# First modulation chunks in four column pieces, the first projection multiplied with them

## The reference

```
mod = silu(c) @ w_ada + b_ada                    # 1024 -> 6 * 1024
shift1, scale1, gate1, shift2, scale2, gate2 = split(mod, 6)
h = rms_norm(x, norm1_g) * (1 + scale1) + shift1
z = h @ w_in                                     # q_a k_a v_a f_a q_b k_b v_b g_a g_b
q_a, k_a, q_b, k_b: rms_norm per head of 64
y_a = attention with forget gates from f_a; y_b = attention with linear biases (8 heads each)
x = x + gate1 * ((sigmoid(g_a) * (y_a @ w_up_fox) + sigmoid(g_b) * (y_b @ w_up_moba)) @ w_out)
h2 = rms_norm(x, norm2_g) * (1 + scale2) + shift2
x = x + gate2 * peer_ffn(h2)                     # 8 heads x 16 experts per token, rows gathered
```

## Time and profile before

| | |
|---|---|
| time, median of 3 runs | 903.43 us (902.26 to 903.75) |
| profiled execution, first to last instruction | 901.5 us |
| mean granted TensorE clock | 0.980 |
| first projection (QA) starts | 31.67 us |
| second projection (VA) starts | 49.42 us |
| attention, VectorE's first partials | 113.73 us |

### The profile page before, as it was taken

The page is one execution under the profiler, slowest core; times in us unless marked ns, Lnnn a source line. Parts: engine busy times, 40 slices in busy tenths (PEclk is TensorE's granted clock), DMA queues, the critical chain, the costliest instruction groups (busy, mean ns, idle before and its releaser), DMA issues.

```text
span 901.5 us, 8445 instructions
## 1 busy us (share of the span) xinstructions
PE 774.0 (86%) x2526; PEld 417.5 (46%) x2526; DVE 613.4 (68%) x1420; ACT 346.4 (38%) x1027; POOL 286.3 (32%) x279
## 2 busy tenths in 40 slices
PE   4999999999999999999997778787777777777777
PEld 2477877667556566565652333233322233222232
DVE  6788798963587977848669788758744444444445
ACT  3458688872243342423423242322422222222222
POOL 4000000000244445453537344453343333333320
PEclk9999999999999999999999989999999999999999
DMA  9978454679399999999999999999999999999994
GB/s 374 422 268 293 165 206 190 251 308 406 109 376 423 418 421 422 416 422 422 420 421 422 421 422 419 422 422 421 423 420 423 420 422 421 421 422 421 422 421 202
DMA packets 44100, 336.70 MB, mean 373 GB/s; under 512 B 4884, under 2 KB 5012, under 8 KB 7320
## 3 DMA queue, kind: packets, MB, share of 16 engines
q0 software_dynamic: 37152, 268.45, 71.8%
q1 hardware_dynamic: 6888, 67.72, 19.1%
q10 hardware_dynamic: 16, 0.00, 0.0%
HBM read 335.11 MB, written 1.05 MB: 373 GB/s over the span
## 4 chain that ended last, share of the span: by engine, by line
PE 49%; DMA 36%; DVE 10%; ACT 3%; issue 2%; SPq 0%; DVEq 0%; ACTq 0%
DMA ring<-in_peer_uv,eid 28%; PE ps_y L1625 21%; PE bank L1595 6%; DMA rows<-in_peer_uv,eid 4%; DMA extra<-in_peer_uv,eid 4%; PE bank L1561 3%; DVE ring L1019 2%; PE bank L1436 2%; PE bank L1438 2%; PE bank L1437 2%; PE bank L1576 2%; PE ps_y L1436 1%; PE ps_y L1438 1%; PE ps_y L1437 1%; PE ps_y L1400 1%
## 5 line engine op out<-in xcount | busy, mean ns | idle before, releaser
L1625 PE MATMUL ps_y<-ring,diag 128*128 128x512 f32 x572 | 275.5, 621 | 57.5 <-ACT diag L1311 57.5
L590 POOL DMA_INDIRECT ring<-in_peer_uv,eid x142 | 156.4, 1102 | 419.8 <-DVE eid L925 228.3
L1019 DVE CUSTOM_DVE_ANT_0 ring<-ring,gates 128x1024 f32<-128x1024 f32 x143 | 173.3, 1225 | 100.4 <-DMA ring<-in_peer_uv,eid 99.7
L1625 PEld LDWEIGHTS ps_y<-ring,diag 128*128 128x128 f32 x572 | 109.4, 197 | 205.5 <-issue 118.8
L1299 ACT ACTIVATE mask<-mask 128x2 f32<-128x2 f32 (+1 forms) x132 | 26.7, 202 | 364.1 <-DVE mask L1019 364.0
L1311 ACT ACTIVATE diag<-ident,mask 128x128 f32<-128x128 f32 x256 | 87.3, 386 | 0.3
L1625 PE MATMUL ps_y<-rows,diag 128*128 128x512 f32 x136 | 63.6, 611 | 9.6 <-ACT diag L1311 9.6
L1304 ACT ACTIVATE mask<-g_sb,mask 128x1 f32<-128x1 f32 x256 | 61.9, 287 | 4.3
L1019 DVE CUSTOM_DVE_ANT_0 rows<-rows,gates 128x1024 f32<-128x1024 f32 x34 | 41.2, 1224 | 31.1 <-DMA rows<-in_peer_uv,eid 31.0
L654 DVE TENSOR_TENSOR w_lo<-ring,w_hi 128x512 fp32r<-128x512 f32 x76 | 50.7, 685 | 11.5 <-PE bank L1438 10.0
L1115 ACT ACTIVATE w_hi<-ring 128x512 fp32r<-128x512 f32 x76 | 45.5, 626 | 24.4 <-PE bank L1438 23.9
(11 more groups left out here) (230 smaller groups left out, 1192.7 us busy)
## 6 DMA issues: line engine op xcount, KB each, us to landing
ring<-in_ada_t SPq DMA_DIRECT2D x11, 2048.0 KB, 9.7
ring<-in_in_t SPq DMA_DIRECT2D x10, 2048.0 KB, 10.3
ring<-in_up_t SPq DMA_DIRECT2D x2, 2048.0 KB, 8.7
ring<-in_out_t SPq DMA_DIRECT2D x2, 2048.0 KB, 13.7
ring<-in_peer_uv,eid POOLq DMA_INDIRECT x142, 28.9
x_sb<-in_x SPq DMA_DIRECT2D x2, 1024.0 KB, 12.1
ring<-in_ada_t SPq DMA_DIRECT2D x2, 1024.0 KB, 21.4
kz<-in_peer_t SPq DMA_DIRECT2D x1, 2048.0 KB, 23.4
```

The source lines that it names most:

```text
L590: pool.indirect_dma_start(uv_row(n), None, peer_uv, bass.IndirectOffsetOnAxis(ap=eid[:, n:n + 1], axis=0)).then_inc(s_uv[name], 16)
L1019: dve.tensor_tensor_reduce(u_row(n), u_row(n), h2[:, n // P, :], 1.0, 0.0, ALU.mult, ALU.add, adot[:, at:at + 1]).then_inc(s_dot, 1)
L1625: ins = pe.matmul(ps_y[:, cut], diag[:, n % ND, :], v_row(n)[:, cut], start=first, stop=last)
```

## The change

The columns of the first four modulation chunks are reordered on the host, so that piece j holds shift1 and scale1 for the k-blocks 2j and 2j+1 of h. A piece is made directly as columns: VectorE now sums 7 k-blocks (6 in the last piece), `piece_sum` turns and sums them with four matmuls that have the partials as stationary operand and one moving column, and `piece_direct` does the remaining k-block (two in the last piece) in the same way from the ring. VectorE reduces the pieces' columns from PSUM and makes `mod` and `a1` for two k-blocks; ScalarE makes those four blocks of h (both tiles) and rounds them. TensorE multiplies them at once with a quarter of QA's weights, all in plain fp32 (`PLAIN = 8`), and the forget logits are accumulated piece by piece in `ps_y`. QA's weights are loaded in four quarters, one behind each modulation chunk; modulation 0 is loaded to slot 3 and modulation 3 follows it there once it is summed. The two scalings of x move from VectorE to ScalarE, two memsets from GpSimd to VectorE. Modulation 4's partials move from QA to KA; modulation 5's from KA to QB (3), KB (3) and VB (2), and its row is summed in attention's step 1. The order of loads behind the head gives modulation 6 the slot of modulation 5.

```diff
-ADA_PE = ((5, 6, 7), (5, 6, 7), (5, 6, 7), (3, 6, 7))
-PLAIN = 4
+PIECE_PE = ((7,), (7,), (7,), (6, 7))
+PLAIN = 8
-ADA_DURING = {QA: 4, KA: 5}
+ADA_DURING = {KA: ((4, 0, 8),), QB: ((5, 0, 3),), KB: ((5, 3, 6),), VB: ((5, 6, 8),)}
+ADA_ROW_AFTER = {QB: 4}
-ADA_LATE = {3: 6, 6: 7, 10: 8, 14: 9, 16: 10}
+ADA_LATE = {1: 5, 3: 6, 6: 7, 10: 8, 14: 9, 16: 10}
...
-    chunks = [("ada", n) for n in range(ADA_FIRST)]
-    chunks += [("z", QA), ("z", VA), ("ada", 4), ("z", KA), ("ada", 5), ("z", QB), ("z", KB), ("z", VB)]
+    pieces = [("ada", 0), ("z", QA), ("ada", 1), ("ada", 2), ("ada", 3)]
+    slot_of = dict(zip(pieces, (3, 0, 1, 2, 3)))
+    chunks = [("z", VA), ("z", KA), ("ada", 4), ("z", QB), ("ada", 5), ("z", KB), ("z", VB)]
     chunks += [("z", 6), ("ada", 6), ("z", 7), ("ada", 7), ("z", 8), ("ada", 8), ("ada", 9), ("z", 9), ("ada", 10), ("ada", 11)]
     chunks += [("up", 0), ("up", 1), ("out", 0), ("out", 1)]
+    slot_of.update(zip(chunks, (1, 2, 3, 0, 1, 2, 3, 0, 1, 2, 3, 0, 1, 2, 3, 0, 1, 2, 3, 0, 1)))
...
+            for j in range(ADA_FIRST):
+                key = ("ada", j)
+                if held_by[key] is not None:
+                    await_chunk_read(sp, held_by[key])
+                for h in range(2):
+                    half = slice(h * KD // 2, (h + 1) * KD // 2)
+                    sp.dma_start(ring[:, slot_of[key], half, :], ada_t[j, :, half, :]).then_inc(s_piece[j][h], 16)
+                two = slice(2 * j, 2 * j + 2)
+                sp.dma_start(ring[:, slot_of["z", QA], two, :], in_t[QA, :, two, :]).then_inc(s_first[j], 16)
...
-            for n in (slice(0, 3), slice(4, 5)):
-                pool.memset(rows[:, n, :], 0.0).then_inc(s_zero, 1)
...
+            for n in (slice(0, 3), slice(4, 5)):
+                dve.memset(rows[:, n, :], 0.0).then_inc(s_zero, 1)
...
+            for j in range(ADA_FIRST):
+                piece(j, 0, PIECE_PE[j][0])
+                if j:
+                    h_low(j - 1)
+                to = columns_of(mod[:], j)
+                parts = len(PIECE_PE[j]) + 1
+                dve.wait_ge(s_summed, j + 1)
+                link(dve.tensor_reduce(to, ps_y[:, 16 * j:16 * j + 4 * parts].rearrange("p (s a k) -> p a k s", a=2, k=2),
+                                       AX_X, ALU.add))
+                link(dve.tensor_tensor(to, to, columns_of(cols[:, 24:24 + 2 * KD], j), ALU.add))
...
+            h_low(ADA_FIRST - 1)
+            low_parts(KD, KD + NLO)
...
+                    for n, first, last in ADA_DURING.get(c_, ()):
+                        m = first + k - (KD - (last - first))
+                        if m >= first:
+                            partials(n * KD + m, n * KD + m + 1)
...
+            for j in range(ADA_FIRST):
+                act.wait_ge(s_a1, j + 1)
+                for k in (2 * j, 2 * j + 1):
+                    for t in range(TILES):
+                        key = ("xT", t, k // 4)
+                        ins = act.activation(hT[:, k, t * P:(t + 1) * P], bank(key)[:, (k % 4) * P:(k % 4 + 1) * P],
+                                             ACT.Identity, scale=a1[:, k:k + 1], bias=mod[:, k:k + 1])
...
+                h_high(j)
...
+            def piece_direct(j):
+                pe.wait_ge(s_piece[j][1], 16)
+                for part, k in enumerate(PIECE_PE[j]):
+                    for m in range(4):
+                        pe.matmul(piece_cols(j, part + 1)[:, m:m + 1], ring[:, slot_of["ada", j], k, m * P:(m + 1) * P],
+                                        silu[:, k:k + 1], start=True, stop=True)
+            def piece_sum(j):
+                pe.wait_ge(s_acc, j + 1)
+                for m in range(4):
+                    ins = pe.matmul(piece_cols(j, 0)[:, m:m + 1], sums_first[:, j % 2, m * P:(m + 1) * P],
+                                    ones[:, 0:1], start=True, stop=True)
+                ins.then_inc(s_summed, 1)
...
+            piece_direct(0)
             for t in range(TILES):
...
+            for j in range(ADA_FIRST):
+                if j:
+                    piece_direct(j)
+                piece_sum(j)
+                if j:
+                    forget_part(j - 1)
+                first_part(j, first_spots)
+            forget_part(ADA_FIRST - 1)
```

More of the change, by code:

```diff
@@ L511, in _ @@
                 sp.dma_start(rows[0:1, r, :], b_ada[0:1, at * D:(at + 1) * D]).then_inc(s_bias, 16)
-            for n in range(ADA_FIRST, len(chunks)):
-                chunk(n)
+            for key in chunks:
+                chunk(key)
             await_block(sp, NZ * KD - 1)
@@ L652, in low_parts @@
                         await_block(dve, j - NLO)
-                    w = ring[:, chunk_no["z", n] % NW, k, :]
+                    w = ring[:, slot_of["z", n], k, :]
                     dve.tensor_tensor(w_lo[:, j % NLO, :], w, w_hi[:, j % NHI, :].bitcast(F32),
                                       ALU.subtract).then_inc(s_w_lo, 1)
[L657 to L665, removed]
-                        continue
[L667 to L672, removed]
@@ L675, in _, with piece @@
-            middle = slice(ADA_FIRST - 1, ADA_FIRST)
-            link(dve.memset(pads, 0.0))
-            link(dve.memset(pads[:, KD, middle], 1.0))
+            def piece(j, first, last):
+                acc = sums_first[:, j % 2, :]
+                for k in range(first, last):
+                    w = ring[:, slot_of["ada", j], k, :]
+                    if k == 0:
+                        dve.wait_ge(s_piece[j][0], 16)
+                        if j >= 2:
+                            dve.wait_ge(s_summed, j - 1)
+                        link(dve.tensor_scalar(acc, w, silu[:, 0:1], None, ALU.mult))
+                        continue
+                    if k == KD // 2:
+                        dve.wait_ge(s_piece[j][1], 16)
+                    ins = dve.scalar_tensor_tensor(out=acc, in0=w, scalar=silu[:, k:k + 1], in1=acc,
+                                                   op0=ALU.mult, op1=ALU.add)
+                    if k + 1 in PIECE_PE[j]:
+                        ins.then_inc(s_acc, 1)
+                    else:
+                        link(ins)
@@ L696, in _ @@
[L696 to L714, removed]
+            inverse_root(D, TILES, s_rstd)
+            for j in range(ADA_FIRST):
[8 more added lines that the diff above has]
+                link(dve.tensor_tensor(to, to, columns_of(cols[:, 24:24 + 2 * KD], j), ALU.add))
+                two = slice(2 * j, 2 * j + 2)
+                dve.scalar_tensor_tensor(out=a1[:, two], in0=mod[:, KD + 2 * j:KD + 2 * j + 2], scalar=1.0,
+                                         in1=cols[:, KD + 2 * j:KD + 2 * j + 2],
+                                         op0=ALU.add, op1=ALU.mult).then_inc(s_a1, 1)
@@ L769, in _ @@
             dve.wait_ge(s_bias, 4 * 16)
[L770 to L774, removed]
+            for c_ in range(VA, NZ_QKV):
+                if c_ == VA:
                     forget_logits()
@@ L1405, in _, with first_part @@
+            def first_part(j, spots):
+                pe.wait_ge(s_first[j], 16)
+                for k in (2 * j, 2 * j + 1):
+                    for t in range(TILES):
+                        h_ready(pe, t, k)
+                        ins = pe.matmul(spots[t], hT[:, k, t * P:(t + 1) * P], ring[:, slot_of["z", QA], k, :],
+                                        start=(k == 0), stop=(k == KD - 1))
+                        if k == KD - 1:
+                            done(ins)
             pe.wait_ge(s_const, 1)
-            pe.wait_ge(s_silu, 2)
+            pe.wait_ge(s_silu, 1)
@@ L1456, in _ @@
             for key in z_order(TILES):
-                if key == "f":
-                    b = fill(key)
-                    for k in range(KD):
-                        ins = pe.matmul(b[0:HEADS, 0:T], wf[:, k, :], hT[:, k, :], start=(k == 0), stop=(k == KD - 1))
-                    done(ins)
-                elif key == "Fcol":
+                if key == "Fcol":
                     pe.wait_ge(s_F, 1)
@@ L1472, in _ @@
                     c_, t = key[1:]
[L1473 removed]
+                    if t or c_ == QA:
                         continue
                     spots = [fill(("z", c_, t))[:] for t in range(TILES)]
[L1476 to L1482 removed]
+                    for k in range(KD):
                         if c_ - 1 in QK and k == KD - 1:
@@ L1682 @@
     at = [0, 1024, 512] + [f_at + 8 + n * 512 for n in range(7)]
+    w_ada = a["w_ada"][0]
+    first = [w_ada[:, at_ + 256 * j:at_ + 256 * (j + 1)] for j in range(4) for at_ in (0, 1024)]
+    w_ada = np.concatenate(first + [w_ada[:, 2048:]], axis=1)
     w_z = np.concatenate([w_in[:, c:c + 512] for c in at], axis=1)
```

203 lines of the change are left out of this document (89 added, 114 removed).

## The result

Slower: four executions took 905.63 to 910.23 us, median 908.6, against 903.21 (902.11 to 903.75) for the kernel before; the ratio is 1.0061, interval 1.0048 to 1.0073, about +5.5 us. A fifth was a disturbed execution, 955.27 us at a granted clock of 0.84, and is not in the ratio. The four have spans of 908.4, 908.2, 903.8 and 905.3: they lie 4.6 us apart, where the five times of the kernel before lie 1.6 apart. The profiled one is the longest of the four, 908.4 against 901.5.

The account below looks back on a forecast made before the run. TensorE was taken to bound the kernel to about 250 us, then DMA. Head -3.2 us (start 44.0 + 2.2 clock = 46.2 against 49.42) plus stall +4.7 gave +1.5: 904.9 us, range 900.6 to 908.8.

Parts of the forecast that it names:

- Slower: Whole kernel: outcome beyond about 0.2% (1.8 us) longer than before, chance 0.10 + 0.28.
- the same: Whole kernel: outcome within about 0.2% (1.8 us) of the time before, chance 0.32 + 0.12.
- (A): The forecast itself: head 3.2 us shorter, attention 4.7 later, 904.9 us, own range 902.5 to 906.5, chance 0.42.
- the stall: Attention step 0: VectorE waits 6.3 us for chunk 6, issued only after chunk 5's last partial; lateness +4.7 us.
- (C): Head: one-column work is dear, every round falls to 1.2 GHz; +5.3 us, 908.7, chance 0.28.
- VectorE's start and the price of one-column work: Head: inverse root done at 10.4 us; one-column matmuls at 0.12 us per instruction.
- Rounds and the start at 44.0 at full clock: Head: rounds end at 17.2, 24.1, 31.0, 38.5; second projection starts at 44.0 if TensorE stays at 2.4 GHz.
- The clock, +2.2: Head rounds: two slow stretches of TensorE at 1.1 us net each, moving the second projection's start to 46.2.
- The rival of dear one-column instructions: Head: a one-column load-and-multiply pair costs 0.19 us, 5 us over 72 instructions; shares the 0.28 chance of (C).
- VectorE's slack and turn of K: Second projection to attention: K's turn in time or 1 us better; last projection ends after 60.3 us, not 62.2.
- (D): Attention: slack pays for the chunk 6 wait, VectorE's 6.3 us shrinking to about 0.5; 900.7 us, chance 0.18.
- What the first 110 us lose reaches the end one to one: Whole kernel: the second part waits for no set time, so gains or losses in the first 110 us carry through.

Follow-up runs that it names:

- extra matmuls: Ten matmuls of 256 moving columns with unread output added on TensorE in the head of the changed kernel; 1.0034 of the kernel before, span 902.3 us.
- the execution whose head stayed at full pace: Profiled execution of the changed kernel with chunk 5's last two partials moved from VB to KB (three beside QB, five beside KB); 0.9971 of the kernel before, span 895.8 us.
- slot swap: Changed kernel with modulation 6 and the second gate chunk exchanging ring slots (8 with 9 behind them); 0.9993 of the kernel before, span 901.7 us.

## Why the prediction was right, and where its sizes were off

The range held at its very edge, the sum did not. The difference measured is +5.5 us where the sum said +1.5: 908.7 on the 903.21 measured beside it, 908.9 on the 903.43 of the forecast, for a range up to 908.8. "Slower" had been given 0.38, less than the 0.44 of "the same". The mechanism of (A) is there, the stall above all, and about half of what (C) says of the clock: the first and third of four rounds were slow in the profile, not every one. That (C)'s figure, +5.3, comes so near is partly luck, as executions of this one kernel lie 4.6 us apart. Two terms were mis-sized, the clock's and the stall's.

- **VectorE's start and the price of one-column work.** Inverse root at 10.4: measured 10.55. One-column matmuls at 0.12: eight took 0.95 at full pace, 1.84 at half. Both right. The working before the first sum was short by half a us: from 13.2 to 16.2 it left 3.0 for the transposes, which had taken 3.62 before and took 3.52.
- **Rounds and the start at 44.0 at full clock.** Right: 43.46 with the extra matmuls, 44.95 in the execution whose head stayed at full pace.
- **The clock, +2.2.** This failed: the profiled execution has +6.1 (50.07 against 44.0). I counted two slow stretches at 1.1 net each, and took the first sum and the first plain part to begin at full pace. They did not. The rounds end at 18.8, 28.3, 35.2 and 44.2, for 17.2, 24.1, 31.0 and 38.5. The first is 1.6 late, by the landing (11.95 for 11.4), the transposes and a sum at half pace, about a third each; the second 4.2, as all of the first plain part ran at half pace (6.58 for 3.67, less VectorE's slack); the fourth 5.7, as the third plain part lost 1.6. Of the 6.1 some 5 are clock, since the execution whose head stayed at full pace started at 44.95. The kernel before went to full pace at 15.68, right after its transposes.
- **The clock from one execution to the next.** By their spans, less the same rest, the other three undisturbed ones would start at 49.9, 45.5 and 47.0 (argued, they have no trace). The mean of the four is 48.1, so that on average the head gains some 1 us on the kernel before, where the forecast said 3.2, and the stall makes the whole of the +5.5; by the timings of the slot swap, 0.9993 with 1 inside its interval, even that gain is not clear of noise.
- **The rival of dear one-column instructions** is ruled out by their 0.12, and with the extra matmuls, 6 us earlier, neither TensorE nor VectorE waits for a chunk's data in the rounds.
- **VectorE's slack and turn of K.** I gave the stretch up to attention 1.9 us less than before; it took 0.9 less. The turn still waited 1.4 us, and the last low part came at 111.65, start + 61.6 instead of 60.6.
- **The stall.** Mechanism, place and cause right: wait 6.63 for a forecast 6.3, issue at 113.03, landing 7.8 later, TensorE held at the first probability transpose. Its lateness was forecast at +4.7 and is +6.3 in the rest: +5.9 at step 1's scores (start + 73.1 for 72.0; before, start + 67.2), of that 1.0 from the point above, and some 0.3 more gathered by 132 us, where TensorE runs at half speed after its stall and chunk 7 is 0.23 late; which of the two it is no run separates. The swap gives all of the 6.3 back.
- **(D), that slack pays for the stall**, is ruled out: the rest went from 852.0 to 858.3, and no step of attention caught up.
- **What the first 110 us lose reaches the end one to one**: right. Step 1's scores come 6.5 us late (123.18 against 116.70), the span is 6.9 longer.

## What to carry to other kernels

When work is spread thinner over a stretch, look at the last piece of it: here two partials of 0.75 us held a ring slot to the end of the last projection, and the queue order put the very next chunk needed behind them, which cost 6.3 us against the kernel before. Follow each moved read to the load that waits for it and to that load's first use. And a chain cut into rounds with thin matmul work in between can't be summed at one clock: price each round at both levels and expect the time to scatter. One profiled execution then does not size such a cause: here two of them said 6.6 us and the repeated timings 2.4.

## What the runs showed of the hardware

- At the start of an execution the record of the granted clock reads 1.00 while instructions run at half pace; only the pace (0.82 against 0.46 us for 512 columns, 6.58 against 3.67 for eight) shows it.
- Plain fp32 instructions with one moving column and 128x128 weights take 0.12 us each in a row (eight in 0.95), less than the 0.192 us of one load, which I had as the upper bound; at half pace they take 0.23 (eight in 1.84). The Trainium skill, "TensorE: Matmul & The Clock Gate", section on LDWEIGHTS, gives a load as its columns over 1.2 GHz, an estimate of 0.85 us for eight; the trace agrees within 0.1 us at full pace with 0.95, but at half pace it shows the double, so a load with its multiply goes with the clock here.
- The same head ran its first plain part in 6.58, 6.13, 6.74 and 3.67 us in four profiles; in the five with extra matmuls ahead it took 3.67. Four of these five had one later part at 4.8 to 5.8 us all the same.
